# Eight places for expert weights, and the last pair's down product half by half

## The reference, cut to what matters

```
hb = jax.nn.silu(xb @ w1[e]) * (xb @ w3[e])      # w1, w3: 1024 x 512
return hb @ w2[e]                                 # w2: 512 x 1024
y = jnp.einsum('nk,nkd->nd', gate, y_assign)
```

## Time and profile before

| what | value |
|---|---|
| median of 3 runs | 1319.6 us (1318.97 to 1320.26) |
| time of the profiled execution | 1319.89 us |
| span of the profiled execution | 1318.1 us |
| PE busy | 1279.4 us, 97% of the span |
| DVE, ACT busy | 699.9 us (53%), 500.4 us (38%) |
| data moved | 363.67 MB, mean 276 GB/s |

### The profile page before, as it was taken

The page is one execution under the profiler, slowest core; times in us unless marked ns, Lnnn a source line. Parts: engine busy times, 40 slices in busy tenths (PEclk is TensorE's granted clock), DMA queues, the critical chain, the costliest instruction groups (busy, mean ns, idle before and its releaser), DMA issues.

```text
span 1318.1 us, 17839 instructions
## 1 busy us (share of the span) xinstructions
PE 1279.4 (97%) x7078; PEld 891.5 (68%) x7078; DVE 699.9 (53%) x1198; ACT 500.4 (38%) x766; POOL 77.7 (6%) x86
## 2 busy tenths in 40 slices
PE   8999999999999999999999999999999999999998
PEld 7987886976675454444454444459956687799986
DVE  5665678667564322223222222257875878755552
ACT  5556574344332111111111111156414585744442
POOL 6730200100000000000000000000000000000000
PEclk9999999999999999999999999999999999999999
DMA  9644648949855999999999999995505335655540
GB/s 352 239 180 164 227 144 299 348 178 340 309 202 222 403 429 426 426 429 428 427 427 427 428 426 429 423 385 175 192 1 206 129 136 158 194 164 180 191 160 33
DMA packets 102212, 363.67 MB, mean 276 GB/s; under 512 B 4098, under 2 KB 28933, under 8 KB 90032
## 3 DMA queue, kind: packets, MB, share of 16 engines
q1 hardware_dynamic: 98656, 352.86, 69.1%
q0 software_dynamic: 3280, 9.58, 2.2%
q10 hardware_dynamic: 192, 0.06, 0.0%
HBM read 361.43 MB, written 1.05 MB: 275 GB/s over the span
## 4 chain that ended last, share of the span: by engine, by line
PE 84%; DVE 8%; ACT 4%; issue 2%; DMA 1%; ACTq 0%; DVEq 0%
PE bank L531 37%; PE bank L924 17%; PE bank L942 8%; PE bank L901 5%; PE bank L1289 5%; PE bank L971 3%; DVE ring_parts L1337 2%; PE bank L932 1%; PE bank L1092 1%; ACT ring_parts L2164 1%; PE bank L585 1%; DMA ring<-in_w_xkv 1%; PE bank L620 1%; PE bank L853 1%; PE bank L925 1%
## 5 line engine op out<-in xcount | busy, mean ns | idle before, releaser
L2164 ACT ACTIVATE ring_parts<-ring 128x1024 fp32r<-128x1024 f32 x234 | 242.6, 1057 | 227.8 <-PE bank L531 200.3
L1337 DVE TENSOR_TENSOR ring_parts<-ring,ring_parts 128x1024 fp32r<-128x1024 f32 x214 | 257.1, 1223 | 131.1 <-ACT ring_parts L2164 128.4
L531 PE MATMUL bank<-ring_parts,arena_parts 128*128 128x512 f32 x1056 | 271.8, 392 | 3.6 <-ACT ring_parts L2164 1.5
L531 PEld LDWEIGHTS bank<-ring_parts,arena_parts 128*128 128x128 f32 x1056 | 196.5, 188 | 48.9 <-ACT ring_parts L2164 2.9
L531 PE MATMUL bank<-arena_parts,ring_parts 128*128 128x256 f32 x1504 | 198.0, 284 | 2.8 <-DVE ring_parts L1337 1.6
L924 PE MATMUL bank<-ring,arena 128*64 128x512 f32 x432 | 192.3, 598 | 7.9 <-issue 7.9
L925 PE MATMUL bank<-ring,arena 128*64 128x512 f32 x448 | 199.6, 599 | 0.0
L531 PEld LDWEIGHTS bank<-arena_parts,ring_parts 128*128 128x128 f32 x1504 | 190.1, 192 | 4.9 <-issue 3.1
L924 PEld LDWEIGHTS bank<-ring,arena 128*64 128x64 f32 x432 | 57.8, 138 | 128.3 <-issue 128.1
L531 PE MATMUL bank<-ring_parts 128*128 128x512 f32 (+1 forms) x624 | 117.1, 346 | 2.1 <-DVE ring_parts L1337 1.2
L531 PEld LDWEIGHTS bank<-ring_parts 128*128 128x128 f32 x624 | 96.6, 190 | 22.1 <-issue 7.9
(11 more groups left out here) (391 smaller groups left out, 1419.6 us busy)
## 6 DMA issues: line engine op xcount, KB each, us to landing
ring<-in_w SPq DMA_DIRECT2D x81, 2048.0 KB, 21.5
ring<-in_w_in SPq DMA_DIRECT2D x27, 2048.0 KB, 9.8
flank<-in_w SPq DMA_DIRECT2D x13, 2048.0 KB, 22.2
ring<-in_w_ada SPq DMA_DIRECT2D x12, 2048.0 KB, 8.6
ring<-in_w_ffn_gate SPq DMA_DIRECT2D x11, 1024.0 KB, 5.4
ring<-in_w_ffn_up SPq DMA_DIRECT2D x11, 1024.0 KB, 8.0
ring<-in_w_ffn_down SPq DMA_DIRECT2D x5, 2048.0 KB, 7.7
ring<-in_w_xkv SPq DMA_DIRECT2D x4, 2048.0 KB, 16.6
```

Source lines behind the costliest of these rows:

```text
L531: mm = pe.matmul(ps[:, o:o + width], *pair, start=(o == 0 and kk == 0 and ha + hw == 0), stop=(kk == kn - 1 and (ha, hw) == terms[-1] and ...
L1337: dve.tensor_tensor(low, src, high, ALU.subtract).then_inc(low_ready, 1)
L2164: act.activation(high, src, ACT.Copy).then_inc(high_ready, 1)
```

## The change

`flank` grows so that it also holds small tensors that are dead by the time the experts start (`work`, `scT`, `wif`, `lam`, `late`, `sheet`, `cols1`, `wroute`). Its first 4096 columns, all four `rows`, become one place, and its next 4096 (`actT` and the small tensors) another: eight places in place of seven. Because `rows[0]` and `rows[1]` are needed later, GpSimd writes one partition of each to memory (`row_stash`) before the place is given to the experts, and broadcasts both back once the first product of `p0` is done. The load of `norm_f_g` moves up to `upped` 30; those of `hy_bias_2` and the kept rows come behind the first product of `p0`. VectorE waits for the kept rows before the filter step of the second block.

The two last units (94 and 95, the w2 of the last pair) don't take the places 6 and 7, which must be given back, but 0 and 1 (`place_of`). They travel whole, in one transfer each, and the ordinary `down` multiplies them: first one half of the output columns, then the other. What has been said of SP's order now reads: units 94 and 95 wait for `down` 30, and `p4x`, `p5x` for `down` 32, `p0`, `p1` for `upped` 31, all in this order.

```diff
-        flank, flank_parts = both("flank", [P, 4 * D + KD * N])
+        TAIL = 4 * D + KD * N
+        flank, flank_parts = both("flank", [P, TAIL + 768 + 3 * 256 + 2 * P + S1_ROWS + KD * (NG + NE)])
...
+        row_stash = nc.dram_tensor("row_stash", (2, D), F32, kind="Internal").ap()
...
-        PLACES = R + 2
+        PLACES = R + 3
...
-            if m == PLACES - 1:
-                return flank[:, 2 * D:2 * D + 4096]
+            if m > R:
+                return flank[:, 4096 * (m - R - 1):4096 * (m - R)]
             return ring[:, R if m == R else (N_BEFORE + FREED[m]) % R, :]
+
+        def place_of(i):
+            return (i if i < WHOLE else i - UNITS) % PLACES
...
-            def down_by_pieces(n):
...
-                    down_by_pieces(n)
+                    down(n)
...
             dve.wait_ge(s["rowsh_in"], 16)
+            dve.wait_ge(s["rows_back"], 16 * 2)
...
-            pool.wait_ge(moe["upped"], 2 * PAIRS)
+            pool.wait_ge(s["rows_g"], 1)
+            for i in range(2):
+                pool.dma_start(row_stash[i:i + 1, :], rows[0:1, i, :]).then_inc(s["rows_kept"], 16)
+
+            pool.wait_ge(moe["upped"], 2 * (PAIRS - 1))
             pool.dma_start(rows[:, 2, :], w["norm_f_g"].rearrange("(a n) -> a n", a=1).broadcast_to([P, D])).then_inc(s["rowf_in"], 16)
+            full(pool, "hy0_0")
+            for i in range(2):
+                pool.dma_start(rows[:, i, :], row_stash[i:i + 1, :].broadcast_to([P, D])).then_inc(s["rows_back"], 16)
             pool.dma_start(rows[:, 3, :], w["hy_bias_2"].rearrange("a o n -> a (o n)").broadcast_to([P, D])).then_inc(s["rowsh_in"], 16)
...
-                if m == PLACES - 1:
+                if m == R + 1:
                     full(sp, "logits")
-                    sp.wait_ge(s["rows_g"], 1)
+                    sp.wait_ge(s["rows_kept"], 16 * 2)
+                elif m == R + 2:
+                    full(sp, "logits")
...
-                    computed(*order[i - PLACES])
-                if i < WHOLE:
-                    expert_load(i % PLACES, 2 * n + u // 3, u % 3)
-            for k in range(KF):
-                for j in range(2):
-                    src = w["w2"][0, NE - 2 + j].rearrange("(p k) n -> p k n", p=P)
-                    sp.dma_start(moe_place((WHOLE + j) % PLACES)[:, k * D:(k + 1) * D], src[:, k, :]).then_inc(last_piece[k], 16)
+                    computed(*order[max(j for j in range(i) if place_of(j) == place_of(i))])
+                expert_load(place_of(i), 2 * n + u // 3, u % 3)
...
-                computed(*max(order[j] for j in range(len(order)) if j % PLACES == last_of[AT[i]]))
+                computed(*max(order[j] for j in range(len(order)) if place_of(j) == last_of[AT[i]]))
```

More of the change, by code:

```diff
@@ L168, in two_blocks @@
         arena, arena_parts = both("arena", [P, 16384])
-        flank, flank_parts = both("flank", [P, 4 * D + KD * N])
+        TAIL = 4 * D + KD * N
+        flank, flank_parts = both("flank", [P, TAIL + 768 + 3 * 256 + 2 * P + S1_ROWS + KD * (NG + NE)])
         rows = flank[:, 0:4 * D].rearrange("p (r n) -> p r n", r=4)
         actT, actT_parts = [f[:, 4 * D:4 * D + KD * N].rearrange("p (k n) -> p k n", k=KD) for f in (flank, flank_parts)]
+        work = flank[:, TAIL:TAIL + 768]
+        scT, wif, lam = [flank[:, TAIL + o:TAIL + o + 256].rearrange("p (k c) -> p k c", k=k) for o, k in ((768, KD), (1024, KD), (1280, 4))]
+        late, sheet = [flank[:, TAIL + o:TAIL + o + P] for o in (1536, 1664)]
+        cols1 = flank[:, TAIL + 1792:TAIL + 1792 + S1_ROWS]
+        wroute = flank[:, TAIL + 1792 + S1_ROWS:].rearrange("p (k c) -> p k c", k=KD)
+        row_stash = nc.dram_tensor("row_stash", (2, D), F32, kind="Internal").ap()
         ident = sb("ident", [P, P])
@@ L175, in two_blocks @@
         upto = sb("upto", [P, P])
-        late = sb("late", [P, P])
         slots = sb("slots", [P, C])
         eps = sb("eps", [P, 1])
-        sheet = sb("sheet", [P, P])
-        cols1 = sb("cols1", [P, S1_ROWS])
         gmoe = sb("gmoe", [P, KD])
@@ L184, in two_blocks @@
         msq = sb("msq", [P, 24, 2])
-        work = sb("work", [P, 768])
-        wif = sb("wif", [P, KD, 32])
-        wroute = sb("wroute", [P, KD, NG + NE])
         rbias = sb("rbias", [P, NG + NE])
@@ L190, in two_blocks @@
         adaT = sb("adaT", [P, 32, 2])
-        scT = sb("scT", [P, KD, 32])
         pick = sb("pick", [P, 2 * H])
@@ L195, in two_blocks @@
         count_i = sb("count_i", [1, 1], I32)
-        lam = sb("lam", [P, 4, 64])
         subg = sb("subg", [P, DV])
@@ L342, in two_blocks @@
         first_piece = [sem(f"first_piece{q}") for q in range(4)]
-        last_piece = [sem(f"last_piece{k}") for k in range(KF)]
         act_chain, dve_chain, pool_chain = sem("act_chain"), sem("dve_chain"), sem("pool_chain")
@@ L349, in two_blocks @@
                      "misc_in norm_hat norm_rms out_stored p_ready qk_ready order_ready pick_ready G2_ready O_ms O_clamped rope_done rope_in "
-                     "route_exp route_in rows1_in rows2_in rowf_in rows_g rowsh_in rowsp_in sheet1_in sheet2_in silu_c "
+                     "route_exp route_in rows1_in rows2_in rowf_in rows_kept rows_back rows_g rowsh_in rowsp_in sheet1_in sheet2_in silu_c "
                      "gut_silu dft_in v_ones pool_low upped wroute_in x0_in x1_in x_new xexp xmax ").split():
             s[name] = sem(name)
-        PLACES = R + 2
+        PLACES = R + 3
         def moe_sems(tag):
@@ L381, in moe_unit @@
                 at = UNITS * n + m
-                return at % PLACES, 16 * (at // PLACES + 1)
-            return m, 16 * (len(range(m, WHOLE, PLACES)) - PAIRS + 1 + n)
+                return place_of(at), 16 * sum(place_of(before_it) == place_of(at) for before_it in range(at + 1))
+            return m, 16 * (sum(place_of(at) == m for at in range(UNITS * PAIRS)) - PAIRS + 1 + n)
         def reach(eng, which, value):
@@ L945, in down @@
                     mm.then_inc(moe["down"], 1)
-            def down_by_pieces(n):
[L949 to L952, removed]
-                for k in range(KF):
-                    pe.wait_ge(last_piece[k], 32)
-                    for half in range(2):
-                        for j in range(2):
[L957 to L961, removed]
             def scatter(n, half):
```

## The result

The changed kernel takes 1329.3 us (median of 7 runs, 1324.5 to 1331.1) against 1320.2 us for the kernel before in the same sessions (1319.0 to 1325.3). By the medians it is 9.1 us slower. The ratio, which is one of means here as in all the experiments, is 1.0059, 95% interval [1.0042, 1.0076], 7.8 us. The forecast was 1323.7 us with a range up to 1327.0, so the sign was right and the size wrong; the median lies 2.3 us above the range. The profiled execution has a span of 1328.8 us against 1318.1, 10.7 us more, a little more than the medians differ.

The account below looks back on a forecast made before the run. Transfers bound the experts from pair 7 on; behind them, the last scatter and `p4x`'s landing decide together. Late load +2.3 and clock +1.8 us make +4.1 on the median 1319.6: 1323.7 us, range 1320.5 to 1327.

Parts of the forecast that it names:

- The eighth place: Experts' stage: each unit lies one queue slot earlier, −4.9 us for each wait from pair 7 on.
- Rival C: Experts' stage: small stops close too, TensorE's pace holds throughout; −6.6 us, 1313.0 us; chance 0.08.
- `norm_f_g` moved up: Experts' stage: its 512 KB load falls in the transfer-bound stretch, +1.2 us on the last pair's units.
- Whole units, half by half: Last down product: TensorE waits 0.4 us for the whole units; the scatter ends some 3 us behind the product.
- One sign of being wrong: Last down product: a wait above 1 us there would mean that the transfer queue broke.
- The stash, the rows back, the small tensors: Before the experts and in the second block: storing rows, broadcasting them back and reading `flank` tensors each cost 0.
- `p4x` behind `down` 32: After the last down product: `p4x` travels alone, takes 8.2 us to land; first matmul 881.5 against 879.23, +2.3 us.
- The clock: Behind the 6.5 us gap ahead of `p4x`: TensorE's clock falls, +1.8 us, bounds 0 and 3.4 us.
- rival A: Before the last pair: wait grows to 2.5 us and the clock falls there too, costing 1.7 us; 1325.0; chance 0.25.
- rival B: At `p4x`: the clock doesn't fall, 1321.9 us, or it lands quickly, down to 1320.8 us; chance 0.15.

Follow-up runs that it names:

- experiment 3: The changed kernel with `norm_f_g` loaded at `upped` 32 again, as before the change: 1327.46 us, ratio 1.0053 to the kernel before.
- experiment 2: The changed kernel with the second block's ring order turned by two, so `p4x` and `p5x` use places 2 and 3: 1318.99 us, ratio 0.9987.
- experiment 5: The changed kernel with six unused matmuls of a constant between the last scatter and `p4x`: 1325.27 us, ratio 1.0032.
- experiment 7: The changed kernel with ring order turned by two and three unused matmuls in the last pair's two waits: 1317.45 us, ratio 0.9970.
- Experiment 4: The kernel before, seven places, with only the last pair's down units loaded whole and multiplied half by half: 1320.58 us, ratio 1.0002.
- experiment 1: The kernel before with one wait added, `p4x` issued only at `down` 32: 1329.95 us, ratio 1.0072.
- experiment 6: The changed kernel with ring order turned by two and `norm_f_g` at `upped` 32: 1316.60 us, ratio 0.9967.
- experiment 8: The changed kernel with ring order turned, `norm_f_g` at `upped` 32 and one unused matmul in each of the last pair's two waits: 1315.12 us, ratio 0.9957.

## Why the prediction was right in sign and wrong in size

Taken from one product to the next in the two profiled executions, in us (forecast, measured):

| step | forecast | measured |
|---|---|---|
| start of the experts' stage (416.90; 418.80) | 0 | +1.9 |
| from there to the last pair's first product | −3.7 | −3.4 |
| from there to the down product (19.2; 21.1) | +0.4 | +1.9 |
| the down product (7.1; 8.8) | 0 | +1.7 |
| from its end to the first matmul of `p4x` (3.8; 10.4) | +5.6 | +6.6 |
| the 48 matmuls of `p4x` (11.2; 13.4) | +1.8 | +2.2 |
| sum | +4.1 | +10.8 (rounded terms: 10.9) |

Without the first row, which is not of the change, the sum is 8.9 us, close to the 9.1 us between the medians.

*The eighth place: right.* It gives one slot of the transfers' queue (5.3 us in experiment 3, for 4.9 booked) and no more; with `norm_f_g` in the stream 3.4 to 4.0 us are left (the changed kernel and experiments 2, 5 and 7). Rival C, that the experts would run at TensorE's pace throughout, is refuted by the waits that remain.

*`norm_f_g` moved up: right in the mechanism, and nearly in size.* The wait ahead of the last pair is 2.0 us longer (3.23 against 1.26) for the 1.2 us booked; in experiments 2 and 5, which carry it too, it is 2.50 and 2.55 us, the 1.2 booked. What it costs in the whole is only visible once the late load is gone: 0.9987 with it, 0.9967 without it, and these intervals, of two sessions, overlap by a little. In the changed kernel the times don't resolve it.

*Whole units, half by half: right.* Experiment 4 gives 1.0002. One sign of being wrong, a wait of over 1 us at the last down product, came true by the number, but not by its meaning: TensorE waited 1.13 us there for VectorE's values (0.93 before), not for a unit.

*The stash, the rows back, the small tensors: right, at nothing.* Places 6 and 7 were loaded from 405.06 on and the DMA engines stood still from 418. Experiment 2 carries all three and isn't slower than the kernel before. The 8.1 us of a broadcast "alone" were misread: at 866 to 874 us the DMA engines were full (share 1.04), and in experiment 3 the same load took 3.5 us. Nothing rests on it.

*`p4x` behind `down` 32: right, and the main cause.* Shown from both sides: the wait alone, put into the kernel before, costs 0.72%, and taking it out of the changed kernel gives back 0.7%, both with the slow matmuls behind the gap. The term was 1 us small: the load landed in 9.1 us here and in 9.6 us in experiment 1, where I took 8.2 from loads that had nothing queued behind them. One of those, the 8.5 us, wasn't into an empty queue either: it was issued at 890.43, while the load issued at 875 to 876 us still had until about 893 (18.1 us from issue to landing). By an estimate from the Trainium skill's figure ("DMA: Bandwidth & Descriptors", "Anatomy of one DMA"; 6.8 us) it would have been 2.3 us small; the measurement disagrees with it by that much.

*The clock: the step that failed.* I booked one fall, for 1.8 us. In the profiled execution the tail had three, and the two that I left out are 3.2 of the 4.8 us that the sum lacks (10.8 less the 1.9 of the first row, less 4.1); the rest, rounded, is the load's 1.0, 0.4 at the block of `p4x` and 0.3 up to the last pair's start.

The fall behind the long gap measured 2.2 us and was foreseen; experiment 5 shows that the idle gap is its cause.

The one ahead of the last pair was rival A, to which I gave a quarter, with "it decides from about 2.5 us on". It came in all three profiles in which `norm_f_g` was moved up and nothing filled the wait (waits of 3.23, 2.50 and 2.55 us), and in neither of the two with `norm_f_g` late (1.26 and 1.08 us, experiments 3 and 6). So it was the likely case. The mechanism was mine; the mistake was to leave it out of the sum.

The third I didn't see at all: two waits of 0.7 and 1.1 us ahead of the down product (0.7 and 0.9 in the kernel before, where the clock stayed up) were followed by a low clock here and in experiment 2, and waits of 0.7 and 1.5 us in experiment 6. But waits of 0.7 and 1.1 us in experiment 5, and of 0.7 and 1.3 us in experiments 3 and 4, were not: three falls in six profiles. In experiments 7 and 8, with one extra matmul there, it didn't come; that fits idle time as its cause, and the clocks of all executions fit it too (the lowest is 0.997 with the extra matmuls, 0.995 and 0.996 without), but two profiles against three in six can't prove it for this wait alone. Why it comes in some executions isn't settled. A fall 20 us ahead isn't what decides: the changed kernel and experiment 2 had one, experiment 6 had none and fell at the down product, experiment 5 had one (granted clock 0.72 over 846 to 852 us) and didn't.

The falls also go with the spread of the changed kernel's seven times, which cover 6.6 us: the two longest (1330.5 and 1331.1 us) have the lowest mean clock, 0.991, and the shortest (1324.5 us, within the stated range) the highest, 0.995.

*What is not of the change.* 1.9 us of the profiled execution arose before the experts: a wait of 2.0 us at 227 us was followed by a low clock, 0.91 over 218 to 236 us:

```profile
218.00:236.00 18.00, 15.96 (x122) 0.91 1.05 388
```

In the profiles of all other kernels here, six of which carry the change, this stretch has 1.00 and the first up product starts between 416.0 and 417.3. So I take it for the chance of one execution.

One slip in the prediction's own numbers: rival B's lower value is 1320.8 us, and the range began at 1320.5. It changes nothing here.

## What to carry to other kernels

When buffers are given out by a formula, write down for each transfer which event frees its place, for the stages behind too. Here the two last units were put into the two places that the next stage wants first, and that alone cost more than the added buffer gave. A place that is free late at the end of a stage should go to the unit that is wanted last in the next one. And where a stage hands over to another, price an idle gap of TensorE at its length and at the slow matmuls behind it, 1.7 to 2.4 us each here. Do so for every wait of the stretch that the change makes longer, not only for the longest. If the gap can't be closed, unused matmuls in it are worth a try: here they cost no time that shows and kept the clock up.

## What the runs showed of the hardware

- Waits far shorter than the gap of 6.9 us were followed by a low clock. Of the waits between the experts' pairs, eight were of 2.5 us or more: 2.53 (kernel before), 3.23 (changed), 2.54 and 2.50 (experiment 2), 2.75 (4), 2.55 (5), 2.65 (6) and 2.70 us (8). Seven were followed by a granted clock of 0.57 to 0.72 over the next four to six microseconds, the one of 2.75 us by 1.00. None of the waits of 0.6 to 2.2 us there was.
- Elsewhere shorter ones were, in some executions: 2.0 us at 227 us (changed kernel), and 0.7 + 1.1 or 0.7 + 1.5 us with only four small transposes between, ahead of the down product (three of six profiles).
- A fall cost 1.7 us at the down product in float32 (8.8 instead of 7.1 us) and 1.7 to 2.4 us at the float32r product behind the long gap (12.83, 13.37 and 13.57 us in experiment 1, the changed kernel and experiment 3, instead of 11.17). Six unused matmuls in the gap kept the clock at 1.00 (experiment 5).
- A load of 2 MB into an empty queue, with others queued right behind it, landed 8.9 to 9.6 us after its issue (experiments 1, 3, 5 and the changed kernel); with none behind it 7.7 us (median of three).
